# One sum of squares per norm on GpSimd, a single ones product behind the first raw unit, and a third raw unit in the accumulators' banks

## What is computed

```python
def rmsnorm(x, g):                       # ten of these, D = 1024
    xf = x.astype(jnp.float32)
    y = xf * lax.rsqrt(jnp.mean(xf * xf, axis=-1, keepdims=True) + EPS)
    return (y * g.astype(jnp.float32)).astype(x.dtype)

def conv_glu_ffn(h, w_gate, w_up, conv_w, conv_b, w_down):    # first block, ffn0 and ffn1
    g = causal_dwconv(h @ w_gate, conv_w) + conv_b
    return (jax.nn.silu(g) * (h @ w_up)) @ w_down

def swiglu(h, w_gate, w_up, w_down):                          # second block, fa0, fb0, fa1, fb1
    return (jax.nn.silu(h @ w_gate) * (h @ w_up)) @ w_down

h = modulate(rms_norm(x, ffn1_norm[l]), sh1, sc1)             # second block: gain and shift of c
```

## Time and profile before

| what | value |
|---|---|
| median of three runs | 1567.77 us |
| span of the profiled execution | 1566.0 us |
| TensorE busy | 1544.7 us, 99% |
| VectorE busy | 1254.6 us, 80% |
| ScalarE busy | 848.0 us, 54% |
| GpSimd busy | 52.4 us, 3% |
| mean granted TensorE clock | 0.998 |

### The profile page before, as it was taken

How to read it: one execution, slowest core, us unless ns; L and a number is a source line. 1 busy time by engine, 2 the same in 40 slices (tenths; PEclk the granted TensorE clock), 3 DMA queues, 4 the chain that set the end, 5 groups by cost and what they waited for, 6 DMA issues and landing times.

```text
span 1566.0 us, 26737 instructions
## 1 busy us (share of the span) xinstructions
PE 1544.7 (99%) x10892; PEld 1434.6 (92%) x10894; DVE 1254.6 (80%) x1588; ACT 848.0 (54%) x1014; POOL 52.4 (3%) x61
## 2 busy tenths in 40 slices
PE   9999999999999999999999999999999999999998
PEld 7989999998799999999999999999999999999997
DVE  7988899787578998978878797887888888785555
ACT  6666555664466545744446664445644456564443
POOL 1000000000010000000000010000000000100000
PEclk9999999999999999999999999999999999999999
DMA  8515886554247885498863358886598844355551
GB/s 297 199 37 181 333 300 249 178 181 139 75 141 296 308 295 182 172 327 315 310 224 139 115 200 322 314 306 226 199 325 307 308 170 165 135 189 188 187 188 67
DMA packets 59805, 344.11 MB, mean 220 GB/s; under 512 B 6800, under 2 KB 7312, under 8 KB 28752
## 3 DMA queue, kind: packets, MB, share of 16 engines
q1 hardware_dynamic: 58752, 340.80, 61.2%
q0 software_dynamic: 544, 1.97, 0.3%
q10 hardware_dynamic: 432, 0.27, 0.1%
HBM read 341.96 MB, written 1.05 MB: 219 GB/s over the span
## 4 chain that ended last, share of the span: by engine, by line
PE 86%; DVE 8%; ACT 3%; issue 2%; DMA 0%; ACTq 0%; DVEq 0%
PE PS L679 25%; PE PS L764 23%; PE PS L680 13%; PE PS L670 8%; PE PS L648 6%; PE PS L734 3%; PE PS L657 3%; DVE wl L1471 2%; DVE Z L1814 1%; DVE XL L1490 1%; PE PS L815 1%; ACT wh L1033 1%; PE PS L709 1%; PE PS L840 1%; DVE RS L1503 1%
## 5 line engine op out<-in xcount | busy, mean ns | idle before, releaser
L1471 DVE TENSOR_TENSOR wl<-raw,wh 128x2048 fp32r<-128x2048 f32 (+2 forms) x256 | 569.8, 2229 | 132.7 <-ACT wh L1033 130.9
L679 PE MATMUL PS<-HP,wh 128*128 128x512 f32 x1728 | 607.4, 395 | 0.0
L1033 ACT ACTIVATE wh<-raw 128x2048 fp32r<-128x2048 f32 (+2 forms) x256 | 475.5, 1859 | 132.0 <-PE PS L764 108.0
L680 PE MATMUL PS<-HP,wl 128*128 128x256 f32 x1728 | 483.6, 280 | 0.0
L679 PEld LDWEIGHTS PS<-HP,wh 128*128 128x128 f32 x1728 | 324.2, 188 | 74.7
L764 PE MATMUL PS<-FX,wh 128*128 128x256 f32 x1920 | 344.7, 281 | 0.0
L680 PEld LDWEIGHTS PS<-HP,wl 128*128 128x128 f32 x1728 | 326.1, 189 | 0.0
L764 PEld LDWEIGHTS PS<-FX,wh 128*128 128x128 f32 x1920 | 295.0, 189 | 2.4
L764 PE MATMUL PS<-FX,wl 128*128 128x256 f32 x960 | 270.0, 281 | 0.0
L764 PEld LDWEIGHTS PS<-FX,wl 128*128 128x128 f32 x960 | 180.9, 188 | 0.0
L1570 DVE SCALAR_TENSOR_TENSOR ada<-ada,AR 128x1024 f32<-128x1024 f32 x144 | 172.9, 1219 | 0.0
(11 more groups left out here) (274 smaller groups left out, 1710.6 us busy)
## 6 DMA issues: line engine op xcount, KB each, us to landing
raw<-weights SPq DMA_DIRECT2D x242, 1024.0 KB, 5.0
ada<-ada_w SPq DMA_DIRECT2D x144, 512.0 KB, 6.3
raw<-weights SPq DMA_DIRECT2D x6, 768.0 KB, 4.3
raw<-weights SPq DMA_DIRECT2D x4, 576.0 KB, 4.9
X<-x SPq DMA_DIRECT2D x2, 512.0 KB, 5.9
raw<-weights SPq DMA_DIRECT2D x2, 512.0 KB, 7.2
out<-Z SPq DMA_DIRECT2D x4, 256.0 KB, 2.4
AR<-c POOLq DMA_DIRECT2D x1, 512.0 KB, 8.9
```

Of the source, the lines that this page charges most:

```text
L679: mm(pairs(bank(bk)), lhsT=lhs(0, k), rhs=HP[:, k], start=k == 0, stop=False, skip_group_check=True)
L680: last = mm(bank(bk, 0, S), lhsT=lhs(1, k), rhs=HH[:, k, :], start=False, stop=k == k_tiles - 1, skip_group_check=True)
L1033: last = A_(dst(wh), src, ACT.Copy)
L1471: last = tt(dst(wl), src, dst(wh).bitcast(F32), ALU.subtract)
```

## The change

GpSimd adds all eight tiles of squares into one, for all ten norms: four pair sums and three accumulating sums. `norm` on TensorE is one product. In an FFN it stands behind all 48 matmuls of the first raw unit and writes bank 3; in a mixer it stands behind the first group of low matmuls of the first unit and writes bank 7. In an FFN the third raw unit goes into banks 0 and 1, the fourth into banks 4 and 5; the waits move with the banks. VectorE makes the second half of h in `part(1, ...)`, behind that part's `g_sum`; ScalarE's list keeps its order.

```diff
-SUM_PARTS = {"fa0": 1, "w0": 1, "fa1": 1, "w1": 1}
+STAT_BANK = {name: 3 for name in FFNS}
+FIRST_BANKS = ((4, 6), (0, 4))
@@ block.gpsimd
-                for c in range(2):
-                    pool.wait_ge(sq_ready, v + c + 1)
+                for c in range(4):
+                    pool.wait_ge(sq_ready, 4 * i + c + 1)
                     pool.tensor_tensor(sq[:, 2 * c, :], sq[:, 2 * c, :], sq[:, 2 * c + 1, :],
                                        ALU.add).then_inc(ev("sq_pair"), 1)
-                pool.wait_ge(ev("sq_pair"), 2 * NORMS.index(name) + 2)
-                pool.tensor_tensor(sq[:, 0, :], sq[:, 0, :], sq[:, 2, :], ALU.add).then_inc(sq_sum, 1)
-                if name not in SUM_PARTS:
-                    for c in (2, 3):
-                        pool.wait_ge(sq_ready, v + c + 1)
-                        pool.tensor_tensor(sq[:, 2 * c, :], sq[:, 2 * c, :], sq[:, 2 * c + 1, :],
-                                           ALU.add).then_inc(sq_sum, 1)
+                    if c:
+                        pool.wait_ge(ev("sq_pair"), 4 * i + c + 1)
+                        pool.wait_ge(sq_sum, 3 * i + c - 1)
+                        pool.tensor_tensor(sq[:, 0, :], sq[:, 0, :], sq[:, 2 * c, :], ALU.add).then_inc(sq_sum, 1)
@@ raw_unit
-                if first:
-                    between()
                 for part in parts:
                     for m in range(2):
+                        if first and first not in STAT_BANK and m == 1 and part == parts[0]:
+                            between()
...
                 last.then_inc(w_used, 1)
+                if first in STAT_BANK:
+                    between()
@@ norm of block.tensor
-                parts = (0, 4, 6) if name not in SUM_PARTS else (0, 4, 5, 6, 7)
-                for i, t in enumerate(parts):
...
-                last.then_inc(stat, 1)
+                pe.wait_ge(sq_sum, 3 * NORMS.index(name) + 3)
+                if name == "mix0":
+                    pe.wait_ge(const_in, 16)
+                mm(bank(STAT_BANK.get(name, 7), 0, S), lhsT=cn("ones"), rhs=cols(WK, 0, KD)[:, 0, :], start=True,
+                   stop=True).then_inc(stat, 1)
@@ ffn of block.tensor
-                raw_unit(n0, 4, shift, first=name, between=lambda: norm(name))
+                raw_unit(n0, FIRST_BANKS[0][0], shift, first=name, between=lambda: norm(name))
+                raw_unit(n0 + 1, FIRST_BANKS[0][1], shift)
+                raw_unit(n0 + 2, FIRST_BANKS[1][0], shift)
+                pe.wait_ge(g_sum, fb + 1)
+                raw_unit(n0 + 3, FIRST_BANKS[1][1], shift)
                 pe.wait_ge(root, NORMS.index(name) + 1)
-                raw_unit(n0 + 1, 6, shift)
-                pe.wait_ge(g_sum, fb + 1)
-                raw_unit(n0 + 2, 4, shift)
-                pe.wait_ge(u_sum, fb + 1)
-                raw_unit(n0 + 3, 6, shift)
+                pe.wait_ge(g_sum, fb + 2)
                 down(n0 + 4, 0, 0, begins=True)
+                pe.wait_ge(u_sum, fb + 2)
@@ part of block.vector (PS[:, 4:6] and PS[:, 6:8] become PS[:, at:at + 2])
                         ins.then_inc(g_sum, 1)
+                        if mid is not None:
+                            mid()
...
                     if late:
                         lo(nu + 3, off)
-                    if mid is not None:
-                        mid()
...
-                part(0, 0, n0, n0 + 1, None, mid=chain[1])
-                part(1, 1, n0 + 2, n0 + 3, n0 + 4)
+                part(0, 0, n0, n0 + 1, None)
+                part(1, 1, n0 + 2, n0 + 3, n0 + 4, mid=chain[1])
```

More of the change, by code:

```diff
@@ L579, in add_squares @@
             def add_squares(name):
-                v, sq = 4 * NORMS.index(name), cols(WK, 0, KD)
-                for c in range(2):
-                    pool.wait_ge(sq_ready, v + c + 1)
+                i, sq = NORMS.index(name), cols(WK, 0, KD)
+                for c in range(4):
+                    pool.wait_ge(sq_ready, 4 * i + c + 1)
                     pool.tensor_tensor(sq[:, 2 * c, :], sq[:, 2 * c, :], sq[:, 2 * c + 1, :],
                                        ALU.add).then_inc(ev("sq_pair"), 1)
-                pool.wait_ge(ev("sq_pair"), 2 * NORMS.index(name) + 2)
-                pool.tensor_tensor(sq[:, 0, :], sq[:, 0, :], sq[:, 2, :], ALU.add).then_inc(sq_sum, 1)
-                if name not in SUM_PARTS:
-                    for c in (2, 3):
-                        pool.wait_ge(sq_ready, v + c + 1)
-                        pool.tensor_tensor(sq[:, 2 * c, :], sq[:, 2 * c, :], sq[:, 2 * c + 1, :],
-                                           ALU.add).then_inc(sq_sum, 1)
+                    if c:
+                        pool.wait_ge(ev("sq_pair"), 4 * i + c + 1)
+                        pool.wait_ge(sq_sum, 3 * i + c - 1)
+                        pool.tensor_tensor(sq[:, 0, :], sq[:, 0, :], sq[:, 2 * c, :], ALU.add).then_inc(sq_sum, 1)
             def zero_keys(l):
@@ L1057, in norm @@
                 act.wait_ge(stat, v + 1)
-                A_(RT[:, 0:S], bank(7, 0, S), ACT.Sqrt, scale=1.0 / D, bias=cn("eps")).then_inc(root, 1)
+                A_(RT[:, 0:S], bank(STAT_BANK.get(name, 7), 0, S), ACT.Sqrt, scale=1.0 / D, bias=cn("eps")).then_inc(root, 1)
                 def half(i):
@@ L1588, in part @@
                         dve.wait_ge(w_used, ng + 1)
-                        ins = tt(pairs(E if conv else C), PS[:, 4:6, 0:S], over(RS[:, 0:S], 2), ALU.mult)
+                        at = FIRST_BANKS[j][0]
+                        ins = tt(pairs(E if conv else C), PS[:, at:at + 2, 0:S], over(RS[:, 0:S], 2), ALU.mult)
                         if not conv:
-                            ins = dve.tensor_reduce(BI[:, 4 * j:4 * j + 2], PS[:, 4:6, S:RW], AX.X, ALU.add)
+                            ins = dve.tensor_reduce(BI[:, 4 * j:4 * j + 2], PS[:, at:at + 2, S:RW], AX.X, ALU.add)
                         ins.then_inc(g_sum, 1)
+                        if mid is not None:
+                            mid()
                     else:
@@ L1614, in part @@
                         dve.wait_ge(w_used, nu + 1)
-                        ins = tt(pairs(G), PS[:, 6:8, 0:S], over(RS[:, 0:S], 2), ALU.mult)
+                        at = FIRST_BANKS[j][1]
+                        ins = tt(pairs(G), PS[:, at:at + 2, 0:S], over(RS[:, 0:S], 2), ALU.mult)
                         if not conv:
-                            ins = dve.tensor_reduce(BI[:, 4 * j + 2:4 * j + 4], PS[:, 6:8, S:RW], AX.X, ALU.add)
+                            ins = dve.tensor_reduce(BI[:, 4 * j + 2:4 * j + 4], PS[:, at:at + 2, S:RW], AX.X, ALU.add)
                         ins.then_inc(u_sum, 1)
```

## The result

The changed kernel takes 1581.3 us (median of four executions, 1580.07 to 1584.72) against 1567.76 us beside it: 1.0091 times as long, with an interval of 1.0079 to 1.0102 (the quotient of the two medians alone is 1.0086). The profiled execution is the longest of the four, 1584.72 us with a span of 1582.8; the span of before was 1566.0. One of the twelve executions of e6 took 1659.86 us at a mean granted clock of 0.85, and no comparison rests on it.

The account below looks back on a forecast made before the run. TensorE, busy 1544.7 of 1566.0 us, was taken as the bound. Terms 5.0 - 0.8 + 0.3 + 4.2 + 0.9 = +9.6 gave a span of 1575.6, with 1.8 us to the median 1577.4; range 1560 to 1584.

Parts of the forecast that it names:

- the stall before the first wide product of ffn0 and ffn1: TensorE would wait some 2 us there for the second `u_sum`, released by VectorE.
- that before the ones product in fa0 and w0: TensorE would wait 2.1 us in fa0 and 2.9 in w0 for GpSimd's last add.
- the reciprocal late against `XL`: VectorE's reciprocal in the norms would come 1 and 2 us later against the first `XL`.
- The rival "faster": GpSimd's adds cost neither side anything; about -10 us, 1558 (1553 to 1564); chance 0.20.
- The rival "no net change": VectorE's delays vanish in idle time before `u_sum` and h, only the sum is late: +1.6, 1569.4; chance 0.13.
- The price of an add: Each GpSimd add among VectorE's `XL` or splits costs VectorE about 0.45 us.
- ffn0 and ffn1: Wide product waits for the later second `u_sum`: 2.5 us late each, +5.0 for both.
- the step from the end of `u_sum` to the wide product: In ffn0, `u_sum` ends at 154.0 and the wide product starts at 154.05.
- the bound of 1.4: Lower bound for each of ffn0 and ffn1: +1.4 us if VectorE is not delayed.
- mix0 and mix1: VectorE's 1.0 us delay shows in full at h in mix1, nothing left over in mix0: together +0.9.
- fa, w and fb: Terms for both norms of each kind: fa +0.3, w +4.2 through late h, fb -0.8 us.
- the 15.2 us: Most the edit can give on TensorE: 12.0 us from 28 removed products plus the holes at `g_sum`.

Follow-up runs that it names:

- e6: Kernel before, with the change's new banks and later second half of h in fa0, fb0, fa1, fb1 alone, sums kept: 1564.81 us against 1567.44, 0.9982.
- e1: Kernel before, with only GpSimd's full sums and the single ones product; banks and second half of h as before: 1583.91 us against 1567.32, 1.0107.
- e8: Kernel before, with 28 more GpSimd adds on a tile of zeros that no engine waits for: 1577.95 us against 1567.51, 1.0069.
- e2: Kernel before, with only the new banks, statistic in bank 3 and later second half of h; sums and ones products as before: 1570.95 us, 1.0024.
- the filled kernel: Changed kernel, with matmuls of zeros without effect where TensorE would stall: 1579.32 us against 1567.44, 1.0077; repeated, 1579.79 us, 1.0087.
- e9: The changed kernel unaltered, measured again beside the filled kernel on one chip: 1585.17 us, 1.0102 times the kernel before.
- e3: Changed kernel, with the second half of h moved back to where the kernel before has it: 1585.33 us, 1.0121 times the kernel before.
- e7: Changed kernel, with VectorE waiting for GpSimd's last sum before the first of two splits: 1584.13 us, 1.0105 times the kernel before.

## Why the prediction was right, and where its sum was short

**The direction and the mechanism** held. Each place that was named is in the trace: the stall before the first wide product of ffn0 and ffn1 (forecast 2 us, 2.24), that before the ones product in fa0 and w0 (2.1 and 2.9, measured 1.9 and 3.05), the last add that begins inside a split, the reciprocal late against `XL` by 1.0 us in ffn0 (2.12 us behind the end of the fourth `XL` in both kernels, and that end 0.96 later) and by 2.1 in w0, fb0 gaining less than 1 us. The rival "faster" fell twice: with e1, and with e8, where adds that nobody waits for cost 10.4 us. The rival "no net change" needed VectorE's delays to vanish before h and `u_sum`; e8 shows 0.6 us or more of loss in each norm.

**The price of an add**, 0.45 us of VectorE, is the step on which most rests. After measures 0.48 in ffn0 (0.96 for two), e8 0.33 to 0.40. Over the whole span VectorE's `XL` and splits, by shape, before and after:

```profile
L1490 DVE SCALAR_TENSOR_TENSOR XL<-X,GM,FX 128x256 fp32r<-128x256 f32 x48 | 25.8, 594 | 0.5 <-ACT FX L1048 0.5
L1471 DVE TENSOR_TENSOR wl<-raw,wh 128x2048 fp32r<-128x2048 f32 x242 | 553.8, 2290 | 130.0 <-ACT wh L1033 128.3
```
```profile
L1480 DVE SCALAR_TENSOR_TENSOR XL<-X,GM,FX 128x256 fp32r<-128x256 f32 x48 | 31.5, 710 | 0.5 <-ACT FX L1038 0.5
L1461 DVE TENSOR_TENSOR wl<-raw,wh 128x2048 fp32r<-128x2048 f32 x242 | 558.0, 2307 | 131.4 <-ACT wh L1023 129.4
```

These two groups alone grow by 9.9 us; VectorE's busy time grows by 13.7 us for 28 adds, 0.49 each.

**ffn0 and ffn1** were put at +2.5 each and are +2.9 with the clock up; their first wide product comes 2.8 us late, counted from the norm's first raw unit (120.89 in before, 121.46 in after, so that all of ffn0 stands 0.57 later). The order of the work was right, ScalarE's and VectorE's, and the delay of `u_sum` was no larger than forecast: it ends at 154.45 instead of 152.34, which is 1.54 later once the 0.57 is taken off, for the 1.65 that were added (1.0 from above and 0.65 for `g_sum`). The term short is the step from the end of `u_sum` to the wide product. It was put at 0.05 us and measures 0.48 (154.45 to 154.93 in after). In e2 it is 0.48 as well (152.61 to 153.09), which is why e2 loses 1.9 us there and not the bound of 1.4, although its `u_sum` is only 0.6 late.

**mix0 and mix1** were put at +0.9 together and are +1.8 filled: in mix1 h is late by the 1.0 that was forecast, but mix0 was taken to have no loss, and it loses 0.7 (0.6 in e8). Why stays open. Two waits for VectorE's `Z` at line 862, 70 us behind the adds, are 1.7 us long in total there and 1.1 in before; but in e6, which has no added add and whose mix0 is 0.5 us shorter than in before, they are 1.7 too, so they do not tell the adds' share.

**fa, w and fb** stand within 0.5 us of their terms with the clock up (+0.8, +4.2, -1.1 for +0.3, +4.2, -0.8). Together the filled kernel is 11.4 to 11.9 us over before, for +9.6.

**The clock** is what the sum left out altogether. It took stalls of 2 to 3 us as costing their own length; in the changed kernel TensorE's clock fell behind five of them in the profiled execution, and those norms are 0.6 to 1.5 us longer than in the filled kernel. It does not fall each time and place, and that is a part of the reason why the executions of e9 lie 6.5 us apart, where those of before lie within 2.1 on any one chip. It is not all of it: 1586.64 and 1580.1 us have mean clocks of 0.994 and 0.995, and 1.5 us of the longer one are the sum that came later in w1. The clock took the time from the middle of the forecast (1577.4) toward the upper end of its range (1584). That the first median stayed inside is owed in part to the width of the range, for this cost had no term in the sum, and in e9 the median stood above it.

**Where the 15.2 us went that the edit could give.** In the span of e1 the 28 products come off, 12.0 us; the adds as such cost 10.1 (e8, waits of 2.7 for GpSimd among them); TensorE waits 17.2 us for the last sum and for `XL`, where before waited 0.2. That is -12.0 + 10.1 + 17.2 = +15.3, and e1 measures +16.5. The two costs overlap in part, and the low clock in six places is not in the sum, so it is a balance of sizes and not a proof of each. As I read it, the ones products that were removed had filled just the time in which GpSimd and VectorE finish. e1 and e2 add up to 20.2 us in the medians and 20.4 in the spans, more than the whole change with 16.8. Of these 3.6 us of span, 1.4 lie in mix0 and 1.2 in fa1, two norms in which the clock fell in e1 and not in after. The third raw unit in its own banks, which hides the `g_sum` hole that the late sum makes larger, can be seen in fb, where it is 0.3.

## What to carry to other kernels

An engine that is idle 97% of the time is not free if its instructions lock out another one: price its work by the growth of the neighbour's instructions in a place where the two already meet, and measure that price with work that nobody waits for, as in e8. A product taken off the busiest engine gives time only if the data that follow are there by then; here the products covered the tail of a chain, and the shorter kernel waits for the same tail. And a stall of 2 us or more on a TensorE that was busy all the time can bring slower microseconds behind it, here 0.6 to 1.5 us each time the clock fell. As it did not fall behind each one, that cost belongs in the range of a forecast, unless something fills the stall.

## What the runs showed of the hardware

- In these traces an add of 0.73 us on GpSimd that comes up while VectorE works in SBUF gets its turn between two VectorE instructions that would follow each other without a gap, and VectorE waits for it: begun inside a 2.3 us split it takes 2.65 us, and with a pair sum at its head the pair of splits takes 5.56 instead of 4.48. The Trainium skill (SBUF — State Buffer, section "Who interferes with whom") calls the shared ports an exclusive lock; the rows agree, and add who is next when both want it: in the norms shown above it was the waiting add.
- Which add meets the split can change from one execution to the next. In e9 it was one add earlier than elsewhere, and the stall 4.43 us instead of 3.
- The granted clock fell from 2.4 to 1.2 GHz for some 3.4 us behind stalls of 1.9 to 3.05 us in a stream of matmuls that is 97% busy. It did not do so behind each: it stayed at 1.0 behind 3.04 us in w0 of e3 and 2.24 us in ffn0 of e7. It also stayed at 1.0 when the gaps were filled with matmuls of zeros, which take nothing from the path.
